# A 31-tap depthwise convolution: from shifted diagonals to four taps stacked on TensorE's rows, in four 32-column tiles

## The chip, the cores and the metric

One core of one Trainium2 chip runs the whole program. The time is the device time of one execution in microseconds, the median of three runs; the profile is one more execution, taken by the hardware profiler.

## The reference

Two transformer-like blocks run over 256 positions (rows) of 1024 channels, all in float32: first a convolution module and a mixture of 16 experts, then attention and a second mixture of experts, then a second block with its own branches. The change sits in the first module, near the start of the program:

```python
def conformer_conv(x, w_pw1, b_pw1, w_dw, b_dw, g, b, w_pw2, b_pw2):
    h = x @ w_pw1 + b_pw1                      # 256 x 1024 -> 256 x 2048
    a, gate = jnp.split(h, 2, axis=-1)
    h = a * jax.nn.sigmoid(gate)
    h = lax.conv_general_dilated(h, w_dw[:, None, :], window_strides=(1,),
        padding=[(CONV_WIDTH - 1, 0)], ..., feature_group_count=D_MODEL) + b_dw   # CONV_WIDTH = 31
    h = jax.nn.silu(layer_norm(h, g, b))
    return h @ w_pw2 + b_pw2                   # 1024 -> 1024
```

The convolution is depthwise: every channel is filtered over time with 31 taps of its own. Nothing behind it can start before it, since the layer norm needs the mean over all 1024 channels.

## The kernel before, in words

Channels lie on the 128 partitions in eight chunks (`c` = 0 to 7), time on the free axis: `hpad[:, c, :]` holds 30 zeros and the 256 gated values of chunk c, `conv[:, c, :]` the result.

Dense products (`split_product`) run in three terms of reduced-precision float32: ScalarE (ACT) copies half a weight block into `w_hi` (`high`), VectorE (DVE) or GpSimd (POOL) makes the remainder `w_lo` (`low`), and TensorE (PE) multiplies high by high, low by high, high by low. `("pw1", kind, half)` are the four blocks of the first matrix, a or g (gate) for channel chunks 0 to 3 (half 0) or 4 to 7 (half 1); PE takes them as a 0, g 0, a 1, g 1. Each block has two row halves `hb`; the third term of row half hb waits for `low(..., hb)`. `gate(half)` is ACT's sigmoid, `glu(half, n)` DVE's product that writes `hpad`; `("pw2", n)` are the blocks of the second matrix.

The 31 taps are shared. DVE does all 31 taps of chunks 0 to 3 and the first 21 of chunk 4 (`tap`: one `scalar_tensor_tensor` of 128 x 256, both tensors in SBUF), the first ten rounds while PE still multiplies block g 1, with the two `low` of that block between them at j = 4 and j = 6. PE does chunks 5, 6, 7 and the last ten taps of chunk 4: for each tap ACT builds a 128 x 128 diagonal matrix (`diagonal`, six buffers), and PE multiplies it with the shifted `hpad` and accumulates in PSUM, 103 matmuls in float32. Then PE averages over the channels (`conv_mean`, eight matmuls with a constant matrix), DVE centres, PE and ACT make the variance, DVE and ACT normalise and apply SiLU, and the product with pw2 follows.

Each engine runs its own instructions in the order written; waits are on semaphores. SP issues the weight loads in the order of the blocks (`stream`, `experts`), POOL loads parameters and the gain rows `rows` of the layer norms, and fetches `shifted` (the attention biases, made in this time too) out of DRAM. The expert stage behind loads 48 blocks of 2 MB, and its loads wait for buffers that the conv stage uses (`conv_over`).

## Time and profile before

| what | value |
|---|---|
| median of 3 runs | 1281.21 us (1279.31 to 1283.12) |
| span of the profiled execution, first to last instruction | 1275.6 us |
| time around the span, taken from the two rows above | 5.6 us |
| PE busy, share of the span | 1195.1 us, 94% |
| DVE, ACT, POOL busy | 50%, 37%, 16% |
| the convolution, from PE's first tap to the end of the channel mean | 63.6 to 112.05 us |

The profiler gives the span of its execution; the time around it is the difference to the median. Times in the views are counted from the start of the span. A float32 matmul leaves two records on PE and two weight loads (PEld), so 103 taps are x206. A row says when a group of instructions started and how long it took from its first start to its last end, how many they were, and in brackets how long the engine had been idle and who ended that.

### The profile page before, as it was taken

The numbers are of one execution on the slowest core, as the hardware profiler recorded it, in microseconds if no ns is written. First come the engines' busy times: TensorE is split into PE (matmuls) and PEld (weight loads), VectorE is DVE, ScalarE is ACT, GpSimd is POOL, SyncE is SP. The second block draws the span as 40 slices with busy tenths as digits, with TensorE's granted clock in tenths as the row PEclk, the third lists the DMA queues.
The fourth block names the chain that finished last, engine by engine and source line by source line (L and its number), as shares of the span: only waits on it lengthen the run. The fifth ranks groups of instructions, "written<-read, shape, count | busy, mean of one in ns | idle before, by whom it ended". The sixth has DMA issues, their size and how long they took to land.

```text
span 1275.6 us, 16095 instructions
## 1 busy us (share of the span) xinstructions
PE 1195.1 (94%) x6536; PEld 854.7 (67%) x6536; DVE 642.8 (50%) x949; ACT 478.1 (37%) x741; POOL 207.0 (16%) x190
## 2 busy tenths in 40 slices
PE   7998999999988998999999988999999889999998
PEld 7986754344435986654444435889887767988996
DVE  3897631212125678712222116596489885445544
ACT  3596421111103466311010113475566534444442
POOL 6000000000002000000000000087788550000000
PEclk9999989999999999789999998999999999999999
DMA  9900879999998531789999993533334342264450
GB/s 332 331 1 1 332 294 431 426 428 428 426 420 280 195 140 59 292 371 427 427 428 427 428 406 130 198 132 133 132 136 176 140 144 79 119 238 159 181 215 33
DMA packets 68162, 321.23 MB, mean 252 GB/s; under 512 B 4071, under 2 KB 12660, under 8 KB 55418
## 3 DMA queue, kind: packets, MB, share of 16 engines
q1 hardware_dynamic: 64944, 308.57, 61.1%
q0 software_dynamic: 2592, 11.42, 2.6%
q8 instruction: 52, 0.85, 0.3%
q10 hardware_dynamic: 554, 0.23, 0.1%
q14 instruction: 20, 0.16, 0.0%
HBM read 317.02 MB, written 3.18 MB: 251 GB/s over the span
## 4 chain that ended last, share of the span: by engine, by line
PE 70%; DVE 15%; DMA 5%; ACT 4%; issue 3%; POOL 2%; DVEq 0%; SPq 0%; ACTq 0%
PE bank L1529 32%; PE bank L1712 23%; PE bank L1594 4%; PE bank L1703 3%; DMA arena<-in_moe_w_up_dram 2%; POOL w_lo L666 2%; DMA ring<-in_w_kv_dram 2%; PE bank L1761 2%; DVE w_lo L666 2%; PE bank L1497 1%; ACT w_hi L953 1%; DVE arena L2298 1%; DVE rows L2852 1%; DVE arena L2871 1%; PE bank L1601 1%
## 5 line engine op out<-in xcount | busy, mean ns | idle before, releaser
L666 POOL TENSOR_TENSOR w_lo<-ring,w_hi 128x512 fp32r<-128x512 f32 (+1 forms) x124 | 178.1, 1469 | 659.3 <-ACT w_hi L953 659.3
L953 ACT ACTIVATE w_hi<-ring 128x2048 fp32r<-128x2048 f32 (+1 forms) x102 | 191.9, 1883 | 213.0 <-PE bank L1529 211.5
L666 DVE TENSOR_TENSOR w_lo<-ring,w_hi 128x2048 fp32r<-128x2048 f32 x71 | 160.8, 2266 | 150.4 <-ACT w_hi L953 149.9
L1529 PE MATMUL bank<-x_hi,w_hi 128*128 128x256 f32 x672 | 112.0, 289 | 3.9 <-DVE x_lo L2253 2.2
L1529 PE MATMUL bank<-x_hi,w_lo 128*128 128x256 f32 x672 | 108.9, 284 | 1.2 <-POOL w_lo L666 1.0
L1529 PE MATMUL bank<-x_lo,w_hi 128*128 128x256 f32 x672 | 108.3, 284 | 0.0
L1529 PE MATMUL bank<-w_hi,x_hi 128*128 128x512 f32 (+1 forms) x336 | 96.7, 403 | 10.8 <-DVE x_lo L2633 3.6
L1712 PE MATMUL bank<-arena 128*64 128x512 f32 x352 | 98.6, 594 | 1.9 <-ACT arena L953 1.8
L1529 PE MATMUL bank<-w_lo,x_hi 128*128 128x512 f32 (+1 forms) x336 | 94.4, 396 | 4.3 <-POOL w_lo L666 4.3
L1529 PEld LDWEIGHTS bank<-x_hi,w_hi 128*128 128x128 f32 x672 | 93.2, 193 | 6.5 <-issue 6.0
L953 ACT ACTIVATE arena<-bank 128x512 f32<-128x512 f32 (+3 forms) x85 | 40.0, 486 | 148.5 <-PE bank L1745 103.9
L2504 DVE TENSOR_TENSOR y_r<-bank,y_r 128x512 fp32r<-128x512 f32 x32 | 22.1, 691 | 143.6 <-ACT y_r L953 143.6
L1529 PEld LDWEIGHTS bank<-x_hi,w_lo 128*128 128x128 f32 x672 | 93.0, 193 | 1.8 <-POOL w_lo L666 1.8
L1529 PE MATMUL bank<-w_hi,x_lo 128*128 128x512 f32 (+1 forms) x336 | 93.6, 394 | 0.0
L1529 PEld LDWEIGHTS bank<-x_lo,w_hi 128*128 128x128 f32 x672 | 93.0, 192 | 0.0
L1712 PE MATMUL bank<-ring,arena 128*64 128x512 f32 x288 | 84.8, 594 | 7.1 <-ACT arena L953 7.1
L1712 PE MATMUL bank<-ring,moe_x 128*64 128x512 f32 x288 | 84.8, 594 | 1.3 <-DMA arena<-in_moe_w_up_dram 1.3
L1529 PEld LDWEIGHTS bank<-w_hi,x_hi 128*128 128x128 f32 x336 | 62.3, 196 | 24.3 <-issue 6.8
L1529 PEld LDWEIGHTS bank<-w_lo,x_hi 128*128 128x128 f32 x336 | 63.7, 195 | 20.3 <-POOL w_lo L666 7.7
L2530 DVE SCALAR_TENSOR_TENSOR arena<-arena,small,bank 128x512 f32<-128x512 f32 x16 | 17.7, 1105 | 116.9 <-PE bank L1712 116.9
L1529 PEld LDWEIGHTS bank<-w_hi,x_lo 128*128 128x128 f32 x336 | 64.5, 196 | 13.4
L2515 DVE TENSOR_TENSOR res<-res,bank 128x512 f32<-128x512 f32 x56 | 34.7, 682 | 74.5 <-PE bank L1761 74.5
(333 smaller groups left out, 1776.9 us busy)
## 6 DMA issues: line engine op xcount, KB each, us to landing
ring<-in_w_in_dram SPq DMA_DIRECT2D x15, 2048.0 KB, 7.8
ring<-in_moe_w_gate_dram SPq DMA_DIRECT2D x12, 2048.0 KB, 20.0
arena<-in_moe_w_down_dram SPq DMA_DIRECT2D x12, 2048.0 KB, 21.8
arena<-in_moe_w_gate_dram SPq DMA_DIRECT2D x12, 2048.0 KB, 17.1
ring<-in_moe_w_down_dram SPq DMA_DIRECT2D x12, 2048.0 KB, 18.4
ring<-in_moe_w_up_dram SPq DMA_DIRECT2D x12, 2048.0 KB, 17.6
arena<-in_moe_w_up_dram SPq DMA_DIRECT2D x12, 2048.0 KB, 21.4
wslots<-in_moe_w_up_dram SPq DMA_DIRECT2D x8, 2048.0 KB, 22.5
```

The source lines that it names most:

```text
L666: last = ops.tensor_tensor(part(w_lo, label, hb)[:, x].bitcast(F32R), ring_half(label, hb)[:, x], part(w_hi, label, hb)[:, x], ALU.subtract)
L953: return s.activation(dst, src, ACT.Copy)
L1497: mm(bank(label)[:, 0:cols], ident[:], moving[:, 0:cols], start=True, stop=True)
L1529: last = mm(bank(use_)[:, at:at + cols], still, moving, start=start and opens and (hb, n, k) == (0, 0, 0), stop=stop and closes and (hb, n ...
L1594: ins = mm(bank(("tap", c))[:, 0:T], diag[:, i % DIAGS, :], hpad[:, c, j:j + T], start=first, stop=last_)
L1601: ins = mm(bank(name)[:, 0:T], mean_w[:], src[:, k, :], start=first and k == channels[0], stop=last_ and k == channels[-1])
L1703: last = mm(b[:, i * width:(i + 1) * width], rows_[:, t, c * P:(c + 1) * P].bitcast(F32R), sel[:, t, :].bitcast(F32R), start=(n, t) == (0, ...
L1712: last = mm(b[half * CAP:(half + 1) * CAP, :], still(k)[:, half * CAP:(half + 1) * CAP], moving(half, k), start=k == 0, stop=k == k_range - 1)
L1761: last = mm(b, sel_T[:, buf, t * P:(t + 1) * P].bitcast(F32R), y[:, h * HALF:(h + 1) * HALF].bitcast(F32R), start=n == 0, stop=n == 1)
L2504: return v.tensor_tensor(y_lo[:, cols].bitcast(F32R), b, y_hi[:, cols], ALU.subtract)
L2515: ins = v.tensor_tensor(res[:, t, cols], res[:, t, cols], b, ALU.add)
L2530: free(v.scalar_tensor_tensor(hidden_rows(hx[:, 0, :]), by_hidden(sg[:, 0, :]), slot_gates[:, u % 2, :], by_hidden(bank(("up", l, u))[:]), ...
```

## The change

Chunks 2 to 7 go to PE, chunks 0 and 1 stay on DVE. PE no longer uses diagonals of 128 channels for one tap: the 128 rows of the array hold four taps (`STACK`) of 32 channels, and one group of 32 channels (g) is computed by one matmul with 32 output columns, written to PSUM partitions 32 g to 32 g + 31. Eight steps q of four taps make 32 taps (the last one zero), four groups g make 128 channels: 32 matmuls for a chunk, 192 in all. For this the moving data must hold the same 32 channels four times, shifted by 0, 1, 2 and 3 positions, on the four quarters of the partitions. SP writes `hpad[:, c, :]` to a DRAM buffer `gated` and reads it back with four DMAs for each chunk. The stationary matrices (128 x 1024 for a chunk, four diagonals of 32 under each other for each q and g) are made by POOL with one `tensor_tensor` each, from `strips` (0/1 pattern) and the tap column `wcol`. ACT's 103 diagonals are gone. The two `low` of the first pw2 block go from behind the channel mean to behind DVE's last tap, POOL's loads of `b2row` and `rows` to behind the last chunk's taps, and `wstack` (the taps in stacked layout) comes in with eight small DMAs and is transposed by PE in two more matmuls. Several semaphores are shared where there were two; nothing else is computed differently.

```diff
-PE_CHUNKS = (5, 6, 7)
-DIAGS = 6
-TAPS_AHEAD = 10
+DVE_CHUNKS = (0, 1)
+PE_CHUNKS = (2, 3, 4, 5, 6, 7)
+TAPS_AHEAD = 16
+STACK = 4
+STRIP = P // STACK
+STEPS = 8
+PADDED = CONV - 1 + T + 2
+REACH = T + STACK * (STEPS - 1)
...
@@ SP
+            stream(0, 3)
+            for q in range(STEPS):
+                n = min(STACK, CONV - STACK * q)
+                sp.dma_start(wstack[q % 4 * STRIP:q % 4 * STRIP + STRIP, q // 4, 0:n * STRIP]...)
+            stream(3, 5)
+            def shift_gated(c):
+                if c > 4:
+                    sp.wait_ge(sem(f"moved{c % 3}"), 16 * STACK)
+                for j in range(STACK):
+                    sp.dma_start(shifted_rows(c)[j * STRIP:(j + 1) * STRIP],
+                                 bass.AP(gated, c * PADDED + j, [[KD * PADDED, STRIP], [STRIP * KD * PADDED, STACK],
+                                                                 [1, REACH]])).then_inc(sem(f"moved{c % 3}"), 16)
+            sp.wait_ge(sem("glu"), 2)
+            keep_gated(2, 2, "gated_even")
+            sp.wait_ge(sem("gated_even"), 16)
+            for c in (2, 3):
+                shift_gated(c)
+            stream(5, moe_n[0])
+            for c, signal in ((4, "gated_even"), (5, "gated_odd")):
+                sp.wait_ge(sem("glu"), c + 1)
+                keep_gated(c, 1, signal)
+            ready(sp, ("pw1", "g", 1, 1))
+            for c in (4, 5, 6, 7):
+                signal = "gated_odd" if c % 2 else "gated_even"
+                sp.wait_ge(sem(signal), 16 * (c // 2 - c % 2))
+                shift_gated(c)
+                if c < 6:
+                    sp.wait_ge(sem("glu"), c + 3)
+                    keep_gated(c + 2, 1, signal)
@@ POOL
+            pool.wait_ge(sem("table_ahead"), 2)
+            freed(pool, "taps")
+            for c in PE_CHUNKS:
+                g.tensor_tensor(stacked(c), strips[:].unsqueeze(1).unsqueeze(1).broadcast_to([P, STEPS, STACK, STRIP]),
+                                wcol[:, :, c, :].unsqueeze(3).broadcast_to([P, STEPS, STACK, STRIP]), ALU.mult)\
+                    .then_inc(sem("stacked"), 1)
             pool.wait_ge(sem("lines"), 16)
...
+            ready(pool, ("tap", PE_CHUNKS[-1]))
+            par(b2row, a["a_b_pw2"].broadcast_to([P, D]), "par_b2")
+            load_rows(0)
+            load_rows(1)
@@ ACT
-            for i in range(DIAGS):
-                diagonal(i)
             highs(("pw1", "g", 1))
             high(("pw2", 0), 0)
             gate(1)
-            for i in range(DIAGS, len(PE_TAPS)):
-                diagonal(i)
...
+            high(("pw2", 0), 1)
+            for c in PE_CHUNKS:
+                tapped(c)
@@ PE
+            for n, c in enumerate(PE_CHUNKS):
+                claim(pe, ("tap", c))
+                pe.wait_ge(sem("stacked"), n + 1)
+                pe.wait_ge(sem(f"moved{c % 3}"), 16 * STACK * (2 if c > 4 else 1))
+                for q in range(STEPS):
+                    for g in range(STACK):
+                        last = mm(bank(("tap", c))[g * STRIP:(g + 1) * STRIP, 0:T], stacked(c)[:, q, g, :],
+                                  shifted_rows(c)[:, g, STACK * q:STACK * q + T], start=q == 0, stop=q == STEPS - 1)
+                full(last, ("tap", c))
+                if n:
+                    freed(pe, ("tap", PE_CHUNKS[n - 1]))
+                    over_channels("conv_mean", conv, (PE_CHUNKS[n - 1],), first=n == 1)
@@ DVE
-            for n in range(4):
+            for n in (2, 3, 0, 1):
                 glu(0, n)
...
             for j in range(TAPS_AHEAD):
                 if j == 4:
                     low(dve, v, ("pw1", "g", 1), 0)
-                if j == 6:
+                if j == 8:
                     low(dve, v, ("pw1", "g", 1), 1)
-                for c in range(4):
+                for c in DVE_CHUNKS:
                     tap(c, j)
```

PE's rows around the convolution, before (the taps are `bank<-arena 128x256`, the mean and variance the row with `mean_w`):

```order
L1529 MATMUL bank<-x_lo,w_hi 128x256 x4
L1529 MATMUL bank<-x_hi,w_lo 128x256 x4
L1594 MATMUL bank<-arena 128x256 x103
L1601 MATMUL bank<-arena,mean_w 128x256 x16
L1610 MATMUL bank<-arena 128x512 x4
L1497 MATMUL bank<-blockmask,ident 128x512 x4
L1529 MATMUL bank<-w_hi,x_hi 128x512 x4
```

and in the changed kernel, where the stationary matrices lie in `rows` and `res` and the shifted data in `arena` and `x_rep`:

```order
L1584 MATMUL bank<-x_hi,w_lo 128x256 x4
L1666 MATMUL bank<-arena,rows 32x256 x64
L1648 MATMUL bank<-arena,mean_w 128x256
L1666 MATMUL bank<-x_rep,rows 32x256 x32
L1648 MATMUL bank<-arena,mean_w 128x256
L1666 MATMUL bank<-x_rep,rows 32x256 x32
L1648 MATMUL bank<-arena,mean_w 128x256
L1666 MATMUL bank<-x_rep,res 32x256 x32
L1648 MATMUL bank<-arena,mean_w 128x256
L1666 MATMUL bank<-arena,res 32x256 x32
L1648 MATMUL bank<-arena,mean_w 128x256 x4
L1648 MATMUL bank<-res,mean_w 128x256 x8
```

103 matmuls of 128 columns have become 192 of 32 columns, and the mean's matmul for a chunk now stands behind the next chunk's taps.

DVE's rows from the first gated product on, before (`L2298` are taps, `L666` the `low` of a block half):

```order
L2280 SCALAR_TENSOR_TENSOR arena<-bank,pcol,arena 128x256 x4
L2287 COPY small<-eps_ln 128x1 x2
L2294 TENSOR_SCALAR arena<-arena,pcol 128x256 x4
L2298 SCALAR_TENSOR_TENSOR arena<-arena 128x256 x12
L666 TENSOR_TENSOR w_lo<-ring,w_hi 128x2048
L2298 SCALAR_TENSOR_TENSOR arena<-arena 128x256 x8
L666 TENSOR_TENSOR w_lo<-ring,w_hi 128x2048
L2298 SCALAR_TENSOR_TENSOR arena<-arena 128x256 x16
L2280 SCALAR_TENSOR_TENSOR arena<-bank,pcol,arena 128x256 x4
L2287 COPY small<-eps_ln 128x1 x2
L2298 SCALAR_TENSOR_TENSOR arena<-arena 128x256 x4
L2294 TENSOR_SCALAR arena<-arena,pcol 128x256
L2298 SCALAR_TENSOR_TENSOR arena<-arena 128x256 x100
```

and in the changed kernel (`L2354` taps, `L689` `low`):

```order
L2336 SCALAR_TENSOR_TENSOR arena<-bank,pcol,arena 128x256 x4
L2343 COPY small<-eps_ln 128x1 x2
L2350 TENSOR_SCALAR arena<-arena,pcol 128x256 x2
L2354 SCALAR_TENSOR_TENSOR arena<-arena 128x256 x6
L689 TENSOR_TENSOR w_lo<-ring,w_hi 128x2048
L2354 SCALAR_TENSOR_TENSOR arena<-arena 128x256 x8
L689 TENSOR_TENSOR w_lo<-ring,w_hi 128x2048
L2354 SCALAR_TENSOR_TENSOR arena<-arena 128x256 x16
L2336 SCALAR_TENSOR_TENSOR arena<-bank,pcol,arena 128x256 x4
L2343 COPY small<-eps_ln 128x1 x2
L2354 SCALAR_TENSOR_TENSOR arena<-arena 128x256 x30
L689 TENSOR_TENSOR w_lo<-ring,w_hi 128x2048 x2
```

Eight taps stand ahead of the first `low` where there were sixteen (the first taps of a chunk are the `TENSOR_SCALAR` rows), 62 taps in all for 145; the last two `low` are those of pw2.

POOL's rows behind its small parameter loads, before:

```order
L877 DMA kg<-in_k_norm_g_dram 128x64
L877 DMA hng<-in_hgrn_norm_g_dram 128x128
L894 DMA rows<-in_ln_mix_g_dram 128x1024
L894 DMA rows<-in_ln_mix_b_dram 128x1024
L894 DMA rows<-in_ln_ffn_g_dram 128x1024
L894 DMA rows<-in_ln_ffn_b_dram 128x1024
L902 DMA arena<-bias_lines 128x8x256 x2
L908 DMA biases<-arena 128x4096
```

and in the changed kernel (the first two rows are the stationary matrices of six chunks):

```order
L941 DMA hng<-in_hgrn_norm_g_dram 128x128
L963 TENSOR_TENSOR rows<-strips,arena 128x1024 x4
L963 TENSOR_TENSOR res<-strips,arena 128x1024 x2
L969 DMA arena<-bias_lines 128x8x256 x2
L941 DMA arena<-in_a_b_pw_dram 128x1024
L957 DMA rows<-in_ln_mix_g_dram 128x1024
L957 DMA rows<-in_ln_mix_b_dram 128x1024
L957 DMA rows<-in_ln_ffn_g_dram 128x1024
L957 DMA rows<-in_ln_ffn_b_dram 128x1024
L980 DMA biases<-arena 128x4096
```

The six products stand ahead of the two reads of `bias_lines`, and the loads of `rows` behind them.

## Rows read from the trace of the kernel before

**Rows 1.** The page: span, and TensorE's busy time.
```profile
span 1275.6 us, 16095 instructions
PE 1195.1 (94%) x6536; PEld 854.7 (67%) x6536; DVE 642.8 (50%) x949; ACT 478.1 (37%) x741; POOL 207.0 (16%) x190
```

**Rows 2.** Chain that ended last, in order: start us, us, what.
```profile
63.56 45.01 PE bank L1594 x206
108.58 3.47 PE bank L1601 x16
...
114.01 5.39 PE bank L1601 x16
...
124.22 2.20 DVE w_lo L666
126.42 1.22 DVE x_lo L2346 x2
...
127.68 11.22 PE bank L1529 x48
```

**Rows 3.** Timeline of DVE, 37 to 63 us: start, us.
```profile
41.24 1.66 DVE L2280 SCALAR_TENSOR_TENSOR arena<-bank,pcol,arena 128x256 f32<-128x256 f32 x4
...
44.36 4.83 DVE L2298 SCALAR_TENSOR_TENSOR arena<-arena 128x256 f32<-128x256 f32 x12
49.11 2.29 DVE L666 TENSOR_TENSOR w_lo<-ring,w_hi 128x2048 fp32r<-128x2048 f32 x1
...
54.49 2.28 DVE L666 TENSOR_TENSOR w_lo<-ring,w_hi 128x2048 fp32r<-128x2048 f32 x1
```

**Rows 4.** Timeline of PE's weight loads and matmuls in block g 1.
```profile
51.45 0.53 PEld L1529 LDWEIGHTS bank<-x_hi,w_lo 128*128 128x128 f32 x4
...
61.62 0.64 PE L1529 MATMUL bank<-x_hi,w_lo 128*128 128x256 f32 x4
```

**Rows 5.** Timeline of ACT: copies of the taps and of the bias line.
```profile
41.71 0.83 ACT L953 ACTIVATE arena<-bank 128x248 f32<-128x248 f32 x2
```

**Rows 6.** Timeline, POOL alone, then POOL and DVE together near 960 us.
```profile
390.73 1.27 POOL L666 TENSOR_TENSOR w_lo<-ring,w_hi 128x512 fp32r<-128x512 f32 x1 [246.60 <-ACT w_hi L953]
...
959.56 5.89 POOL L666 TENSOR_TENSOR w_lo<-ring,w_hi 128x512 fp32r<-128x512 f32 x4
...
961.49 2.82 DVE L2852 SCALAR_TENSOR_TENSOR rows<-rows,pcol 128x255 f32<-128x255 f32 x2
```

**Rows 7.** Groups of POOL by form, and its timeline: the shortest and the most broken patterns.
```profile
L666 POOL TENSOR_TENSOR w_lo<-ring,w_hi 128x68 fp32r<-128x68 f32 x4 | 1.2, 320 | 355.9 <-ACT w_hi L953 355.9
...
3.16 0.71 POOL L864 TENSOR_SCALAR_AFFINE_SELECT blockmask<-ones 128x128 f32<-128x128 f32 x1
...
11.46 0.29 POOL L864 TENSOR_SCALAR_AFFINE_SELECT blockmask<-ones 128x128 f32<-128x128 f32 x1
```

**Rows 8.** Windows: us, busy of PE, PEld, DVE, ACT, POOL, then the granted clock.
```profile
115.10:118.60 3.50, 3.50 (x11) 2.76 (x10) 2.16 (x2) 0.56 (x1) 0.00 (x0) 0.51 0.00 0
```

**Rows 9.** Timeline and chain: matmuls with 64 columns, and with 128 columns.
```profile
192.45 0.61 PE L1712 MATMUL bank<-ring,arena 128*64 128x512 f32 x1 [0.89 <-ACT arena L953]
...
192.45 0.64 PE L1712 MATMUL bank<-arena 128*64 128x512 f32 x1
...
175.25 13.91 PE bank L1712 x64
...
119.23 3.60 PE L1610 MATMUL bank<-arena 128*128 128x512 f32 x8
```

**Rows 10.** DMA issues: KB each, us from issue to landing.
```profile
out_dram<-res SPq DMA_DIRECT2D x2, 512.0 KB, 2.7
...
arena<-bias_lines POOLq DMA_DIRECT2D x2, 1024.0 KB, 8.0
```

**Rows 11.** Timeline of ACT in the normalisation: the second of four roundings.
```profile
125.22 0.63 ACT L953 ACTIVATE x_hi<-arena 128x512 fp32r<-128x512 f32 x1
```

**Rows 12.** The chain at the end of the first expert stage.
```profile
363.30 25.01 DMA ring<-in_w_kv_dram
```

More of the change, by code:

```diff
@@ L151, in program @@
         w_lo = [sb(f"w_lo{i}", [P, BLK // 2]) for i in range(2)]
+        with nc.sbuf_tensor("x_rep", [P, 3, STACK, REACH], F32) as x_rep:
+            pass
         x_hi = sb("x_hi", [P, KD, T])
@@ L186, in program, with shifted_rows, stacked @@
         wdw = take(CONV * KD)
+        wcol = take(STEPS, KD, STACK)
+        rep_first = take(2, STACK, REACH)
+        assert take.at[0] <= 3 * BLK
+        def shifted_rows(c):
+            return rep_first[:, c - 2] if c < 4 else x_rep[:, c - 4] if c < 7 else rep_last[:, 0]
+        def stacked(c):
+            where = (rows[0][:, 0, :], rows[0][:, 1, :], rows[1][:, 0, :], rows[1][:, 1, :], res[:, 0, :], res[:, 1, :])
+            return where[c - 2].rearrange("p (q g m) -> p q g m", q=STEPS, g=STACK)
         take = carve(3 * BLK)
@@ L325, in program @@
         over_any = [sb(f"over_any{l}", [1, 1], I32) for l in range(LAYERS)]
+        gated = nc.dram_tensor("gated", (P, KD, PADDED), F32, kind="Internal")
         lines = nc.dram_tensor("bias_lines", (2 * HEADS, BIAS_LINE), F32, kind="Internal")
@@ L1576, in _ @@
             for n in range(2):
-                last = tr(bank("taps")[:, n * 124:(n + 1) * 124], wst[0:124, n, :], ident[0:124, 0:124])
+                tr(bank("taps")[:, n * 124:(n + 1) * 124], wst[0:124, n, :], ident[0:124, 0:124])
+            pe.wait_ge(sem("par_stack"), 16 * STEPS)
+            pe.wait_ge(sem("hpad0"), 3)
+            for n in range(2):
+                last = tr(bank("taps")[:, (2 + n) * P:(3 + n) * P], wstack[:, n, :], ident[:])
             full(last, "taps")
@@ L2320, in _ @@
             for j in range(TAPS_AHEAD, CONV):
-                for c in range(4):
+                for c in DVE_CHUNKS:
                     tap(c, j)
-                tap(4, j - TAPS_AHEAD)
-            dve.wait_ge(sem("conv_tap"), DVE_TAPS)
-            ready(dve, ("tap", 4))
-            free(v.tensor_tensor(conv[:, 4, :], conv[:, 4, :], bank(("tap", 4))[:, 0:T], ALU.add), ("tap", 4))
-            freed(dve, ("tap", 4))
+            low(dve, v, ("pw2", 0), 0)
+            low(dve, v, ("pw2", 0), 1)
             ready(dve, "conv_mean")
@@ L2333, in _ @@
                 ins.then_inc(sem("conv_centred"), 1)
-            low(dve, v, ("pw2", 0), 0)
             dve.wait_ge(sem("conv_centred"), 4)
```

117 lines of the change are left out of this document (48 added, 69 removed).

## The prediction

> **What bounds the kernel now.** I read the page first: PE is busy for 1195.1 of 1275.6 us [rows 1]. So a change pays where it takes time out of PE's own queue, or out of a wait there. Then the chain that ended last, for the place of the change: it lies on PE. From 63.56 us PE works 45.01 us on the taps, 206 records for 103 matmuls, 0.437 us each, then 3.47 us on the channel mean [rows 2]. The end of the mean at 108.58 + 3.47 = 112.05 us is what I compare below; everything behind it hangs on it. Third, the timelines of DVE and PE ahead of the taps. PE's product g 1 stands between two suppliers: its third term begins at 51.45 us, right when DVE's `low`, begun at 49.11 us for 2.29 us, is ready, and its last matmuls end at 61.62 + 0.64 = 62.26 us [rows 3, 4]. So that `low` has no slack before the change either. That is the place to watch.
>
> **The taps on PE.** The change removes 49.8 us (62.26 to 112.05) of waiting, taps and mean. It puts in 192 matmuls of 32 columns on four column tiles. The trace has none of these; it has matmuls of 64 columns on two tiles. There the first matmuls of the two tiles start at the same 192.45 us, and a pair of products, 64 records, takes 13.91 us: 32 matmuls of 512 columns, 0.435 us each. With the full width the same form takes 3.60 us for 8 records, 0.90 us each [rows 9]. So two column tiles truly run side by side. If four do too, a step q costs the 0.43 us of one matmul: 48 x 0.43 = 20.6 us. If only two did, it would be 192 x 0.43 / 2 = 41.3 us. I take 20.6, since the only tiled row scales fully, and keep 41.3 as the far end. With the eight matmuls of the mean (3.5 us) the stretch is 24.1 us, so 25.7 us less than 49.8.
>
> A rule speaks for a dearer value: the Trainium skill (TensorE: Matmul & The Clock Gate, Part 3 on packing small matmuls) gives 2.38 times for three column tiles, 79% of full scaling; by it, as an estimate, the taps would cost 20.6 / 0.79 = 26 us and the sum would be 5.5 us higher. No row here shows three or four tiles; the two-tile rows show no such loss.
>
> **The stationary matrices on POOL.** Six `tensor_tensor` of 1024 columns. POOL alone takes 1.27 us for 512 columns [rows 6] and 0.32 us for 68 [rows 7], so 2.14 ns a column, and 2.37 us for 1024. The pattern is broken into 32 runs of 32; the first mask (64 runs) takes 0.71 us where the last (one run) takes 0.29 [rows 7], 7 ns a run, so 0.2 us more: 2.6 us. The far end is that mask's 5.5 ns a column, 5.7 us. I take 2.6, the same operation. They start when ACT has copied the taps, 41.71 + 0.83 = 42.54 us [rows 5].
>
> By themselves they are hidden: 6 x 2.6 us end at 58, and PE wants the first at 62. But DVE works beside them on operations with two SBUF tensors. Near 960 us the same two engines meet: four POOL operations take 5.89 us, 1.47 each instead of 1.27, and two DVE `scalar_tensor_tensor` of 255 columns take 2.82 us, 1.41 each [rows 6], where a tap of this form takes 4.83 / 12 = 0.40 [rows 3]. I read that as turns: one DVE operation gets in between two POOL operations, and each waits for the other. With POOL operations twice as long, DVE then does one tap per 2.6 + 0.2 = 2.8 us, not seven. Operations that read PSUM are not of this kind, so the gated products (from 41.24 us, 1.66 us for four [rows 3]) pass.
>
> The sum on DVE: POOL is done at 42.54 + 2.6 + 5 x 2.8 = 59.1 us. By then DVE has five taps. Taps 6, 7, 8 need 1.2 us, and `low` for g 1 another 2.3 us: ready at 62.6 us. PE stands in its third term from 51.45 us until then: **+11.1 us**. In the queue behind it are all of g 1, the taps and the mean. DVE's second `low` comes 3.2 + 2.3 us later, at 68.1, when PE is 4.8 + 1.0 us into the rest: just in time. The two added transposes of the taps on PE (under 0.5 us) vanish in this wait.
>
> After a wait PE's clock falls: behind the gap at 112 us the granted clock is 0.51 for 3.5 us [rows 8], the lower level of 1.2 GHz, and sixteen records take 5.39 us where sixteen of the same form took 3.47 [rows 2]. The longer wait here will do the same once: **+1.9 us**. Block g 1 ends at 62.26 + 11.1 + 1.9 = 75.3 us, then **-25.7 us** for the stretch: the mean ends at 99.4 us, not 112.05.
>
> **Input through DRAM.** For each chunk SP issues one write and four reads of 147 KB. 512 KB take 2.7 us to land in a quiet stretch [rows 10]. Chunks 2 and 3 go out at about 42.5 us, early. Chunk 4 waits for the first gated product of half 1, behind DVE's 32 taps: 62.6 + 3.2 + 2.3 + 16 x 0.40 = 74.5 us; write 2.7, reads issued 1.6 and landed 2.7 later: 81.5 us. PE has chunks 2 and 3 until 75.3 + 6.9 = 82.2 us. Cost nothing, with under 1 us to spare. Chunks 5 to 7 follow about every 2 us and PE takes 3.9 us for each. If that cover went, a landing of 8.0 us as `bias_lines` had under load [rows 10] in both directions would cost 10 us. DVE's last 30 taps (12.1 us from 77) and the two `low` (4.6 us) end near 94, ahead of the mean's last part.
>
> **ACT, and behind the mean.** ACT's 103 diagonals fed PE's taps and delayed nothing else; taking them out is worth nothing of its own. Behind the mean one `low` of 2.20 us stands on the chain at 124.22, and PE starts 1.22 us after it at 127.68 [rows 2]; with it gone, DVE's second remainder follows ACT's rounding at 125.22 + 0.63 us [rows 11] and is done near 126.5: **-1.1 us**. The loads for the expert stage start with the layer norm's end and PE's progress and move along; where that stage ends on its queue (25.01 us of DMA on the chain [rows 12]) the queue has moved as well, so the gain is kept.
>
> **Sum.** 11.1 + 1.9 - 25.7 - 1.1 = -13.8 us. The profiled span of 1275.6 us becomes 1261.8; with the 5.6 us between span and median, 1281.2 - 13.8 = **1267.4 us**.
>
> **The rivals.**
> - *DVE is not held by POOL*, or gets more than one turn: then `low` is ready before 50 us, g 1 ends at 62.7 with the two transposes, and chunk 4's data land at 61.7 + 2.7 + 1.6 + 2.7 = 68.7, ahead of PE's 69.6. The mean ends at 86.8: -25.2 - 1.1, **1254.9 us**. For it: the row near 960 us is another stage. Against it: its two engines run the same kinds of operation.
> - *Column tiles run two at a time*: +20.7 us, **1288.1 us**, slower than before. It decides from 0.72 us for a step of four on, where 0.43 is full scaling. For it: more than two are not shown. Against it: both start within one record, with nothing lost.
> - *POOL's broken pattern is dear*: each 1 us of its price costs 6 us; from 4.9 us on the gain is gone, and at 5.7 us the time is **1286 us**.
> - *The way through DRAM is late*, or the tiles scale by three quarters: 5 to 10 us more, **1272 to 1278 us**.
>
> **How the numbers follow.** Forecast 0.57 (its own range 1262 to 1272), no hold 0.16, late data or partly scaled tiles 0.14, two tiles at a time 0.08, dear POOL 0.05. Leaving out the last two, the range is 1254 to 1279 us. The measurement tells about 0.3%, 4 us, from no change. Faster by more: 0.57 + 0.16 + nearly all of 0.14 and little else, 0.86; within it 0.03; slower 0.11.
>
> **What would show it.** The third term of g 1 starts near 62.6 us, its PE wait named by DVE's `w_lo`; DVE's taps last 2.5 us and more while POOL makes the matrices, 0.48 us after; POOL's six take 2.6 to 2.8 us each; a chunk's 64 records on PE take 3.4 us; a granted clock of 0.5 for some 3.5 us once g 1 goes on; no wait on `x_rep` from DMA beyond 1 us. Taps at 0.48 us throughout would break the largest term; 7 us for a chunk would break the gain; a wait of PE for DMA at chunk 4 would move the loss to the DRAM route.

## The result, and the profile after

The changed kernel takes 1264.47 us in the median of four runs (1263.55 to 1264.67); the kernel before, run on the same chip beside it, takes 1280.26 us (1279.02 to 1283.12). The ratio is 0.987, with a 95% interval of 0.986 to 0.989: 15.8 us less. The forecast was 1267.4 us, 13.8 us less.

The page after, to be set against [rows 1]:

```profile
span 1262.9 us, 16324 instructions
...
PE 1178.5 (93%) x6716; PEld 829.4 (66%) x6716; DVE 619.0 (49%) x866; ACT 441.4 (35%) x642; POOL 218.9 (17%) x198
```

The span falls from 1275.6 to 1262.9 us, 12.7 us, and PE's busy time by 16.6. The profiled execution after has a device time of 1264.65 us, 1.75 us around its span. In the executions of the kernel before that were timed beside the experiments, 1.7 to 2.7 us lie around the span. So the 5.6 us "around the span" in the table before were in good part scatter: the profiled execution before was a quick one, some 2 to 3 us below the median. That is also most of the step from 12.7 us between the traces to 15.8 us between the medians. The sums below are made from span to span, as the prediction's was.

The timelines of DVE and POOL while the stacked matrices are made (start us, us, engine, line, operation, how many), against [rows 3]:

```profile
42.63 7.81 POOL L963 TENSOR_TENSOR rows<-strips,arena 128x1024 f32<-128x1024 f32 x4 [22.59 <-ACT arena L1025]
50.41 4.14 POOL L963 TENSOR_TENSOR res<-strips,arena 128x1024 f32<-128x1024 f32 x2
...
43.90 2.72 DVE L2350 TENSOR_SCALAR arena<-arena,pcol 128x256 f32<-128x256 f32 x2
46.54 9.08 DVE L2354 SCALAR_TENSOR_TENSOR arena<-arena 128x256 f32<-128x256 f32 x6
55.54 2.28 DVE L689 TENSOR_TENSOR w_lo<-ring,w_hi 128x2048 fp32r<-128x2048 f32 x1
...
60.91 2.28 DVE L689 TENSOR_TENSOR w_lo<-ring,w_hi 128x2048 fp32r<-128x2048 f32 x1
63.12 6.42 DVE L2354 SCALAR_TENSOR_TENSOR arena<-arena 128x256 f32<-128x256 f32 x16
```

Two windows of about 4 us show the exchange (busy time and number of PE, PEld, DVE, ACT, POOL, those at the edges counted in, then the granted clock): three operations of DVE for three of POOL, then eleven where POOL is silent.

```profile
50.55:54.50 3.95, 1.10 (x10) 0.90 (x8) 3.95 (x3) 1.62 (x1) 3.95 (x3) 1.00 1.03 284
63.20:67.20 4.00, 4.00 (x36) 4.00 (x35) 4.00 (x11) 1.92 (x1) 0.00 (x0) 1.00 0.17 60
```

POOL's six products take 11.9 us, about 2.0 each, and DVE's taps keep step with them, where from 63.12 us on a tap takes 0.40 us. POOL's operations are shorter than forecast (2.0 us instead of 2.6), so `low` is ready at 57.8 us and not at 62.6.

The timeline of PE, against [rows 2] and [rows 4]; the bracket is the idle time before the group and who ended it:

```profile
57.88 1.23 PE L1584 MATMUL bank<-x_hi,w_lo 128*128 128x256 f32 x4 [6.23 <-DVE w_lo L689]
...
70.23 7.11 PE L1666 MATMUL bank<-arena,rows 128*32 128x256 f32 x128
...
77.90 3.66 PE L1666 MATMUL bank<-x_rep,rows 128*32 128x256 f32 x64
...
97.68 3.69 PE L1648 MATMUL bank<-res,mean_w 128*128 128x256 f32 x16 [1.53 <-ACT res L1150]
...
108.61 1.21 PE L1584 MATMUL bank<-w_hi,x_hi 128*128 128x512 f32 x4 [0.37 <-DVE x_lo L2397]
```

The wait for `w_lo` is there, 6.2 us long. Between the taps there is no wait for the transfers. The chain gives the parts of the stretch without overlap:

```profile
70.30 7.04 PE bank L1666 x128
77.34 0.63 PE bank L1648 x2
77.97 3.59 PE bank L1666 x64
...
94.22 1.94 PE bank L1648 x8
```

The mean is done at 94.22 + 1.94 = 96.16 us, 15.9 us earlier than the 112.05 of before (forecast 99.4). A window over the wait and what follows (busy time of PE, PEld, DVE, ACT, POOL, then the granted clock, the DMA share and GB/s) shows the price of the pause:

```profile
51.00:65.00 14.00, 7.77 (x52) 7.57 (x51) 14.00 (x19) 2.01 (x2) 5.32 (x4) 0.76 0.94 314
```

The last place to read is late. The two programs are the same from the layer norm on, yet the lead is not kept:

| place, on PE | before | after | lead |
|---|---|---|---|
| end of the mean | 112.05 | 96.16 | 15.9 |
| first product of pw2 | 127.68 | 108.61 | 19.1 |
| first expert product | 175.25 | 156.11 | 19.1 |
| third pair of expert products | 220.52 | 203.14 | 17.4 |
| last mixing of the first expert stage | 391.70 | 375.90 | 15.8 |
| next dense product | 406.29 | 393.63 | 12.7 |

Two pairs of expert products ran in part at the lower clock (15.65 and 15.38 us instead of 13.95), which is nearly all of the first 3.3 us. The other 3.1 us are lost in one place. Here are the same instructions of the kernel before and then of the one after, the 16 warming matmuls in front of the next layer norm's transposes:

```profile
391.70 2.11 PE L1761 MATMUL bank<-y_r,selT_r 128*128 128x512 f32 x8 [1.99 <-DVE y_r L2504]
394.38 7.13 PE L1497 MATMUL bank<-blockmask,ident 128*128 128x512 f32 x16 [0.57 <-DVE res L2515]
402.19 1.07 PE L1645 MATMUL bank<-ident,xtok 128*128 128x128 f32 x8 [0.67 <-DVE xtok L2405]
```

```profile
375.90 2.10 PE L1815 MATMUL bank<-y_r,selT_r 128*128 128x512 f32 x8 [1.61 <-DVE y_r L2555]
381.38 8.80 PE L1552 MATMUL bank<-blockmask,ident 128*128 128x512 f32 x16 [3.38 <-issue]
390.01 1.91 PE L1699 MATMUL bank<-ident,xtok 128*128 128x128 f32 x16
```

Before, the warming matmuls follow 0.57 us behind the mixing and are over when the transposes' data arrive at 402.19. After, PE stands still for 3.38 us with no releaser ("issue"). The matmuls then take 8.80 us instead of 7.13: the granted clock reads 1.00 when they start and 0.53 from 382.4 to 386.0 us. The transposes wait behind them: the data of the first ones had been there since 386.6 us, of the others since 388.0.

### The profile page after: what moved, and what is told of

Read it like the earlier page. It is cut to its first block, busy times and chain, and to the rows that moved or that the text cites. A ratio compares the mean times of both kernels' runs of the same rounds, so it can differ in the third digit from the quotient of the medians.

```text
span 1262.9 us, 16324 instructions
## 1 busy us (share of the span) xinstructions
PE 1178.5 (93%) x6716; PEld 829.4 (66%) x6716; DVE 619.0 (49%) x866; ACT 441.4 (35%) x642; POOL 218.9 (17%) x198
## 4 chain that ended last, share of the span: by engine, by line
PE 72%; DVE 15%; ACT 5%; issue 3%; DMA 3%; POOL 2%; DVEq 0%; SPq 0%; ACTq 0%
PE bank L1584 34%; PE bank L1766 25%; PE bank L1757 3%; DMA arena<-in_moe_w_up_dram 2%; PE bank L1815 2%; POOL w_lo L689 2%; PE bank L1666 2%; DVE w_lo L689 1%; PE bank L1552 1%; ACT w_hi L1025 1%; DVE rows L2903 1%; DVE arena L2581 1%; DVE arena L2922 1%; DVE arena L2354 1%; PE bank L1799 1%
## 5 line engine op out<-in xcount | busy, mean ns | idle before, releaser
L689 POOL TENSOR_TENSOR w_lo<-ring,w_hi 128x512 fp32r<-128x512 f32 (+1 forms) x124 | 178.1, 1469 | 663.9 <-ACT w_hi L1025 663.9
L689 DVE TENSOR_TENSOR w_lo<-ring,w_hi 128x2048 fp32r<-128x2048 f32 x71 | 160.8, 2267 | 149.2 <-ACT w_hi L1025 148.7
L1766 PE MATMUL bank<-arena 128*64 128x512 f32 x352 | 103.3, 613 | 1.9 <-ACT arena L1025 1.8
L1766 PE MATMUL bank<-ring,arena 128*64 128x512 f32 x288 | 87.9, 606 | 7.1 <-ACT arena L1025 7.1
L1025 ACT ACTIVATE arena<-bank 128x512 f32<-128x512 f32 (+4 forms) x86 | 40.3, 486 | 148.5 <-PE bank L1799 103.5
```

Source lines behind the costliest of these rows:

```text
L689: last = ops.tensor_tensor(part(w_lo, label, hb)[:, x].bitcast(F32R), ring_half(label, hb)[:, x], part(w_hi, label, hb)[:, x], ALU.subtract)
L1025: return s.activation(dst, src, ACT.Copy)
L1766: last = mm(b[half * CAP:(half + 1) * CAP, :], still(k)[:, half * CAP:(half + 1) * CAP], moving(half, k), start=k == 0, stop=k == k_range - 1)
```

## The experiments

Each is an edit of the changed kernel. A shift of 1.5 to 2.7 us can lie over all times of one execution, because the six records of PE's first three warming matmuls (at 11.3 us, 17.3 us in experiment 8) took 2.81 us in some executions and 4.3 to 5.5 us in others; where it matters I say so. Where it comes from stands in the last section.

**1. The low parts first.**

```diff
-                if j == 4:
+                if j == 0:
                     low(dve, v, ("pw1", "g", 1), 0)
-                if j == 8:
+                if j == 1:
                     low(dve, v, ("pw1", "g", 1), 1)
```

> Edit: both low(pw1,g,1) stand ahead of nearly all of VectorE's taps (the first at tap 0, the second after two taps) instead of after 8 and 16. Theory A (GpSimd's six products hold VectorE's taps, and what TensorE waits for is only the low part queued behind eight held taps): TensorE's idle 6.2 us before the first x_hi,w_lo matmuls of pw1 g1 is under 1 us, half 1 of pw1 g ends near 62.5 instead of 70.3, and the clock stays at 1.00 through it. But VectorE still has its 32 taps ahead of the gates of half 1, so these come near 68.3 (69.5 now); with 0.5 us to the write, 2.5 us for it, and 4 us for issue and read, chunk 4's rows land near 74 to 75 while TensorE is done with chunks 2 and 3 at 69.6. So TensorE waits some 4 to 5 us there, and the mean comes only about 3 us earlier: near 1261.5 us. Theory B (the DRAM route has slack to spare, or the wait is given back nowhere): the whole 7.8 us, near 1256.7. Theory C (POOL holds VectorE whatever the order is, the low part itself comes late): no gain, 1264.5.

1266.89 us (1264.14 to 1272.69), ratio to the kernel before 0.989 (0.986 to 0.992). The timeline of DVE, then of PE:

```profile
46.61 3.88 DVE L689 TENSOR_TENSOR w_lo<-ring,w_hi 128x2048 fp32r<-128x2048 f32 x1 [2.57 <-ACT w_hi L1025]
50.42 3.92 DVE L2350 TENSOR_SCALAR arena<-arena,pcol 128x256 f32<-128x256 f32 x2
54.26 4.00 DVE L689 TENSOR_TENSOR w_lo<-ring,w_hi 128x2048 fp32r<-128x2048 f32 x1
58.18 11.96 DVE L2354 SCALAR_TENSOR_TENSOR arena<-arena 128x256 f32<-128x256 f32 x30
70.06 1.65 DVE L2336 SCALAR_TENSOR_TENSOR arena<-bank,pcol,arena 128x256 f32<-128x256 f32 x4
```

```profile
63.30 7.11 PE L1666 MATMUL bank<-arena,rows 128*32 128x256 f32 x128
77.26 5.81 PE L1666 MATMUL bank<-x_rep,rows 128*32 128x256 f32 x64 [6.21 <-DMA x_rep<-gated]
```

The taps start at 63.30 instead of 70.23 us: what PE had waited for was only the low part's place behind held taps, as theory A says. And the wait comes back at chunk 4, 6.2 us for the rows out of DRAM. That was to be 4 to 5 us; the gates come at 70.06 and not at 68.3 because the low parts are held too, 3.9 us each instead of 2.28. Behind the wait the chunk takes 5.81 instead of 3.66 us, so the mean ends at 95.66 + 1.99 = 97.7 us, 1.5 later than in the changed kernel. Theories B and C fall. The gain of about 3 us that I expected is not there: in the trace it is a loss of 1.5 us, in the times no difference (the intervals overlap).

**2. The low parts first, and fewer taps ahead of the gates.**

```diff
-TAPS_AHEAD = 16
+TAPS_AHEAD = 8
```
(and the edit of experiment 1)

> Edit: as the run before, and TAPS_AHEAD is 8 instead of 16, so that VectorE does 16 taps and not 32 before the gates of half 1. Theory A: the gates come near 62 to 63, chunk 4's rows land near 68.5, before TensorE asks for them at 69.6; VectorE's remaining 46 taps of 0.40 us end near 83 to 84, before the mean asks at 88. The mean ends near 88.3 instead of 96.15, all of 7.8 us is kept: near 1256.7 us. Rival: if it is the writes and reads through DRAM, not VectorE's queue, that makes TensorE wait in the run before, the wait at chunk 4 stays over 3 us and the time stays near 1261.

1260.61 us (1257.40 to 1263.86), ratio 0.984 (0.981 to 0.987). PE's timeline:

```profile
11.22 4.73 PE L1552 MATMUL bank<-xtok,ident 128*128 128x512 f32 x6 [1.57 <-DVE x_lo L2301]
...
65.08 7.11 PE L1666 MATMUL bank<-arena,rows 128*32 128x256 f32 x128
...
72.92 3.66 PE L1666 MATMUL bank<-x_rep,rows 128*32 128x256 f32 x64
...
89.17 1.99 PE L1648 MATMUL bank<-arena,mean_w 128*128 128x256 f32 x8
```

No wait over 0.2 us is left between the taps, so it was DVE's queue ahead of the gates that made the rows late. The mean ends at 91.2 us, 5.0 earlier than in the changed kernel although this execution lost 4.73 - 2.81 = 1.9 us at its start: 6.9 of the 7.8 us expected. The times show less than the trace: the median lies 3.9 us above the 1256.7 us expected, and its interval still touches that of the changed kernel (0.986 to 0.989).

**3. POOL's products in halves.**

```diff
-                g.tensor_tensor(stacked(c), ...)
+                for h in range(2):
+                    steps = slice(h * STEPS // 2, (h + 1) * STEPS // 2)
+                    ins = g.tensor_tensor(stacked(c)[:, steps], ...)
```

> Edit: GpSimd builds each stacked matrix in two products of 512 columns instead of one of 1024 (12 in all); nothing else. Theory A (VectorE passes by turns, one of its instructions for each of GpSimd's): GpSimd's total stays near 11.8 us (12 of 0.98), VectorE's taps in that stretch take about 1.1 us each instead of 2.1, the eight ahead of the low part are done near 52 to 52.5 instead of 55.5, the low part near 54.8, TensorE's wait is 3.2 instead of 6.2 us and the time about 3 us less: near 1261.5. Rival (VectorE is held in proportion to GpSimd's busy time, whatever the size of its instructions): the taps stay at 2.1 us, the low part at 57.8, no change within 0.5 us of 1264.5. Third: a fixed cost of an instruction of GpSimd of 0.5 us or more would lengthen its total to 17 us, and the stacked matrices would still be early enough (needed from 70.3 on).

1262.91 us (1260.46 to 1270.04), ratio 0.988 (0.984 to 0.992): the time alone tells nothing. The timelines do:

```profile
42.47 8.94 POOL L966 TENSOR_TENSOR rows<-strips,arena 128x512 f32<-128x512 f32 x8 [20.35 <-ACT arena L1028]
...
45.65 7.22 DVE L2357 SCALAR_TENSOR_TENSOR arena<-arena 128x256 f32<-128x256 f32 x6
52.79 3.13 DVE L689 TENSOR_TENSOR w_lo<-ring,w_hi 128x2048 fp32r<-128x2048 f32 x1
```

```profile
55.97 1.22 PE L1587 MATMUL bank<-x_hi,w_lo 128*128 128x256 f32 x4 [4.49 <-DVE w_lo L689]
```

Six taps take 7.22 us, 1.2 each, where a held tap took 2.0, and the first eight of POOL's halves 1.12 us each. The taps follow the length of POOL's instruction, as turns do, so the rival falls. The low part begins 2.75 us earlier, but it is now itself among POOL's work (3.13 us instead of 2.28): PE's wait is 4.49 us, between the two expected values.

**4. The order of the tiles.**

```diff
-                for q in range(STEPS):
-                    for g in range(STACK):
+                for g in range(STACK):
+                    for q in range(STEPS):
```

> Edit: in each chunk the loops over the column tiles and the steps are swapped: eight matmuls in a row on one 32-column tile, then the next, instead of the four tiles in turn. The matmuls are the same. Theory T (the 0.11 us a matmul of the 4-tile taps comes from four neighbouring matmuls running at once on different tiles): in a row on one tile each takes the 0.43 us that a full-width matmul of 256 columns takes; a chunk goes from 3.5 to 13 to 14 us, six chunks from 21 to some 80, and the time rises by about 58 to 62 us, to near 1325. Rival (a matmul of 32 columns is just cheaper by itself, its price goes with the stored columns): no change, 1264.5. Between: overlap only at the changes of tile, 3 of 31, near 1320.

1311.22 us (1309.24 to 1313.19), ratio 1.024 (1.020 to 1.028). PE's timeline:

```profile
70.05 21.98 PE L1666 MATMUL bank<-arena,rows 128*32 128x256 f32 x128
...
92.59 11.50 PE L1666 MATMUL bank<-x_rep,rows 128*32 128x256 f32 x64
```

The same 32 matmuls take 11.50 instead of 3.66 us when neighbours share a tile. That is the overlap of the four tiles, a factor of 3.1 (3.5 if the three changes of tile in this order overlap fully), and the rival falls. Over six chunks 68.0 us instead of 21.4 are 46.6 more, and the time rose by 46.8. My 58 to 62 us were too much: in a row on one tile a 32-column matmul takes 0.36 us (0.40 if the three changes of tile overlap fully), not the 0.437 of a full-width tap [rows 2].

**5. The mean behind all taps.**

```diff
             for n, c in enumerate(PE_CHUNKS):
                 ...
-                if n:
-                    freed(pe, ("tap", PE_CHUNKS[n - 1]))
-                    over_channels("conv_mean", conv, (PE_CHUNKS[n - 1],), first=n == 1)
             pe.wait_ge(sem("conv_tap"), DVE_TAPS)
-            over_channels("conv_mean", conv, DVE_CHUNKS)
+            over_channels("conv_mean", conv, DVE_CHUNKS, first=True)
+            for c in PE_CHUNKS[:-1]:
+                freed(pe, ("tap", c))
+                over_channels("conv_mean", conv, (c,))
```

> Edit: the mean's matmuls of chunks 2 to 6 stand behind all the taps instead of between them. Theory S (each change between 32-column tiles and full-width matmuls costs time: two matmuls of the mean took 0.63 us between chunks and eight in a row 1.94, which is 0.49 for two, and a chunk of taps behind a mean 3.59 instead of 3.52): the stretch from the first tap to the mean's end, 25.9 us now, is 21.1 of taps and 3.9 of 16 mean matmuls, 25.0: 0.9 us less. Rival (the 0.63 is only where the modelled ends fall, nothing is lost at a change): 25.9 as before, within 0.1. Either way the time of the whole, 1264.5, moves by less than its noise of some 2 us; the stretch in the trace decides.

1264.95 us (1263.46 to 1266.53), ratio 0.988 (0.986 to 0.991). PE's timeline:

```profile
73.44 7.11 PE L1666 MATMUL bank<-arena,rows 128*32 128x256 f32 x128
...
94.30 3.72 PE L1648 MATMUL bank<-arena,mean_w 128*128 128x256 f32 x16
```

From the first tap to the mean's end are 98.02 - 73.44 = 24.6 us instead of 25.9: 1.3 us less, where 0.9 was expected. The taps take 20.9 instead of 21.4 us and the mean 3.7 instead of 4.5. A change between 32-column tiles and full width costs time on both sides. (This execution lost 2.7 us at its start.)

**6. The low parts of pw2 back behind the mean.** The edit puts `low(("pw2", 0), 0)` behind the centring and `low(("pw2", 0), 1)` behind the normalising, where the kernel before has them:

```diff
-            low(dve, v, ("pw2", 0), 0)
-            low(dve, v, ("pw2", 0), 1)
             ready(dve, "conv_mean")
             ...
+            low(dve, v, ("pw2", 0), 0)
             dve.wait_ge(sem("conv_centred"), 4)
             ...
+            low(dve, v, ("pw2", 0), 1)
```

> Edit: the two low parts of pw2's first block go back to where the kernel before had them, one behind the centring, one behind the normalising. Theory 1 (the prediction's term): the first one lies in VectorE's 3.1 us of waiting for the deviation and costs nothing, the second stands ahead of the first x_lo and delays pw2's first split matmul (108.6 now) by 1.1 to 1.4 us; the variance matmuls stay at 3.7 us for 16 at a clock of 1.00, because the gap ahead of them is 1.5 us in both. Theory 2 (the move is also what kept the clock up at the variance): the 16 variance matmuls go back to 5.4 us and pw2 starts 3 us later. The time: 1265.7 by the one, 1267.5 by the other.

1266.58 us (1264.20 to 1270.38), ratio 0.990 (0.987 to 0.992). PE's timeline:

```profile
98.91 3.69 PE L1648 MATMUL bank<-res,mean_w 128*128 128x256 f32 x16 [1.53 <-ACT res L1150]
...
110.89 1.21 PE L1584 MATMUL bank<-w_hi,x_hi 128*128 128x512 f32 x4 [1.42 <-DVE x_lo L2397]
```

pw2's first product waits 1.42 instead of 0.37 us: 1.05 us is what the move is worth, close to the 1.1 of the prediction. The variance still takes 3.69 us, so theory 2 falls.

**7. All three edits** (experiments 2 and 5 together).

> Edit: the low parts first, 16 VectorE taps ahead of the gates instead of 32, and the mean behind the taps, together: the candidate for a version better than both. From the second run's profile, whose mean ended at 91.16 in an execution that began 1.8 us late on TensorE, minus 0.9 if the changes of tile cost what theory S says: the mean ends at 90.3 with that late start and at 88.5 without. Against 96.15 that is 5.9 to 7.7 us less, and the time, 1260.6 in the second run, would be 1257 to 1260.

1260.94 us (1257.11 to 1267.57), ratio 0.988 (0.984 to 0.991), the profiled execution with a span of 1255.4 us. PE's timeline:

```profile
73.50 7.15 PE L1666 MATMUL bank<-x_rep,rows 128*32 128x256 f32 x128 [1.43 <-DMA x_rep<-gated]
...
87.67 3.72 PE L1648 MATMUL bank<-arena,mean_w 128*128 128x256 f32 x16
```

The mean ends at 91.4 us with a late start of 1.9, against 90.3 expected, and the median lies just above the 1257 to 1260 us expected. The gain of experiment 5 is gone into a new wait: without the mean's matmuls between chunks PE asks for chunk 4's rows sooner, and waits 1.43 us for them.

**8. More instructions ahead on PE.** 24 matmuls of 16 columns on the identity, results unused, before the input has landed:

```diff
+            claim(pe, ("x", 0))
+            for _ in range(24):
+                mm(bank(("x", 0))[:, 0:16], ident[:], ident[:, 0:16], start=True, stop=True)
             pe.wait_ge(sem("x_in"), 16)
```

> Edit: 24 matmuls of 16 columns on the identity before the input has landed, in TensorE's first 6 us of idle time, so that all of its later instructions lie further on in its program; nothing else. The question is the 2.9 us for which no releaser shows in the first layer, behind the last expert and the branch over the spill (ahead of the 16 warming matmuls at 381.4), which all five profiles of the changed program have (2.8 to 3.8 us) and the one of before has not. Theory F (it hangs on where the code behind the branch lies): the idle time changes clearly, to under 1 us or to more than 4, and the warming matmuls run at full clock, 7.1 instead of 8.8 us, if it goes. Theory G (it hangs on what the DMA queues or the other engines do at that time): it stays at 2.8 to 3.8 us. The time: 1264.5 if it stays, some 1261 if it goes. The added matmuls hide behind the 6 us wait for the input and cost nothing; if the first transposes run at a higher clock for them, a further 1 us goes.

1269.22 us (1267.64 to 1272.27), ratio 0.992 (0.990 to 0.995). PE's timeline:

```profile
1.78 10.42 PE L1612 MATMUL bank<-ident 128*128 128x16 f32 x48 [1.78 <-POOL ident L901]
...
383.55 7.13 PE L1552 MATMUL bank<-blockmask,ident 128*128 128x512 f32 x16 [0.57 <-DVE res L2569]
```

The matmuls do not hide: 48 records at 0.217 us are 10.4 us, and pw2 starts 5.9 us later than in the changed kernel. But the stall is gone: 0.57 us and 7.13 us, to the hundredth as before the change, and of the 5.9 us only 2.1 are left at the next dense product (395.74 against 393.63).

**9. The same with 9 matmuls.**

> Edit: as the run before with added matmuls, but 9 of them instead of 24. In that run the 24 matmuls came to 48 instructions of 0.217 us, 10.4 us and not under 6, which pushed everything up to pw2 back by 5.9 us; of the 5.9 only 2.1 were left at 395 us, because the 2.9 us of idle time ahead of the warming matmuls was gone (0.57 us, as before the change) and these ran in 7.1 instead of 8.8 us. With 9, 18 instructions of 0.217 us end at 5.7 us, before the input at 6.1: no delay. Theory F1 (any sufficient shift of the code behind the branch removes the stall, 36 instructions of weights and matmuls with it): idle 0.57 us, all behind it 3.6 us earlier, near 1261. Theory F2 (the shift is too short, or the 96 instructions of the other run were needed to cross a boundary): the stall stays at 2.8 us and the time at 1264.5. Theory G (the stall went in that run because of the 4 to 6 us shift in time against the transfers, and not in code): it stays too, so only its going tells F1 from both others.

1265.54 us (1264.20 to 1266.62), ratio 0.987 (0.986 to 0.989). PE's timeline:

```profile
382.41 8.80 PE L1552 MATMUL bank<-blockmask,ident 128*128 128x512 f32 x16 [4.30 <-issue]
```

The stall stays, and with it the time of the changed kernel. So not every shift of the code removes it, or it was the shift in time that did it in experiment 8.

**10. The best version that the runs suggested:** the low parts first, `TAPS_AHEAD = 6`, the mean behind the taps, and the 9 matmuls of experiment 9.

> Edit: the low parts first, 12 VectorE taps ahead of the gates (TAPS_AHEAD 6; with 16 ahead TensorE waited 1.4 us for chunk 4's rows once the mean stood behind the taps), the mean behind the taps, and the 9 added matmuls of the run beside this one. Expected: gates 1.6 us earlier than with 8 ahead, no wait at chunk 4, the mean's end at 88.5 (full clock from the start) to 90.5; and, if the stall ahead of the warming matmuls goes, 3.6 us more behind it. The time: 1257 to 1259 without the last, 1253 to 1256 with it; before was 1279 to 1281 and the changed kernel 1264.5.

1258.59 us (1257.55 to 1263.22), ratio 0.982 (0.981 to 0.984), an interval that lies below that of the changed kernel. The time is in the 1257 to 1259 us expected for a stall that stays. PE's timeline:

```profile
74.04 7.11 PE L1669 MATMUL bank<-x_rep,rows 128*32 128x256 f32 x128 [1.90 <-DMA x_rep<-gated]
...
376.26 8.80 PE L1552 MATMUL bank<-blockmask,ident 128*128 128x512 f32 x16 [2.87 <-issue]
```

Both hopes behind this version failed: the stall stays, and PE still waits 1.90 us at chunk 4, though the first gates come 1.5 us earlier (63.86 instead of 65.38 in experiment 7). In the groups of DMA issues the writes `gated<-arena` of this stretch now take 4.2 us to land (median of four), 3.3 in experiment 7, and SP issues chunk 4's reads at 69.28 instead of 68.85 us: what DVE gains, the writes lose.

**11. The 24 matmuls inside PE's own wait.** They stand in the changed kernel's 6.2 us of idle time, in front of the third term of g 1:

```diff
+                        if n == 2 and (label, hb, opening) == (("pw1", "g", 1), 0, True):
+                            freed(pe, ("pw1", "a", 0, 0))
+                            for _ in range(24):
+                                mm(bank(("pw1", "a", 0, 0))[:, 0:16], ident[:], ident[:, 0:16], start=True, stop=True)
                         if n == 2 and opening:
                             pe.wait_ge(lo_made[hb], ...)
```

> Edit: the 24 added matmuls of 16 columns (48 instructions on TensorE) stand in the changed kernel's 6.2 us of idle time ahead of the first x_hi,w_lo of pw1's g1, instead of ahead of the input. They take 0.1 us each there at full clock, 5 us, so nothing is put back, but all code behind them lies exactly as far on as in the run with 24 that lost the 2.9 us stall, and the times of the transfers are those of the changed kernel. Theory F2 (where the code lies decides, and 9 more matmuls were too few): idle ahead of the 16 warming matmuls 0.57 us instead of 3.4, these at 7.1 instead of 8.8 us, pw2's products of the next stage from 390.0 instead of 393.6. Theory G (it was the 6 us shift in time against the transfers): the stall stays at 2.8 us or more. Beside it: if TensorE is kept busy through the wait, the clock stays at 1.00 and the half of pw1's g1 behind the wait takes 10.8 instead of 12.4 us; taps begin at 68.7 instead of 70.3. The time: 1264.5 minus 1.6 for the clock, minus 3.6 more by F2: near 1259.5, or near 1263 by G.

1265.17 us (1259.72 to 1267.64), ratio 0.987 (0.984 to 0.990). PE's timeline:

```profile
53.46 7.78 PE L1581 MATMUL bank<-ident 128*128 128x16 f32 x48
...
376.63 3.43 PE L1819 MATMUL bank<-y_r,selT_r 128*128 128x512 f32 x8 [1.99 <-DVE y_r L2559]
379.98 7.34 PE L1552 MATMUL bank<-blockmask,ident 128*128 128x512 f32 x16
```

The stall is gone again, with the last mixing at 376.63 us where the changed kernel has 375.90. A shift in time against the transfers, 0.7 us here, does not explain it, for the last mixing starts at 376.12 us in experiment 6, where the stall stays. The code's place is left, theory F2. The gain by it does not show in the time: the matmuls took 7.78 us instead of 5 and delayed the taps (74.13 us, with a late start of 1.9).

The second expectation of this run failed, and says more than the first. PE was busy through the whole former wait, and its granted clock fell all the same: it reads 1.00 until 56.2 us and 0.50 from there to 66.4. The added records follow each other every 0.112 us before that and every 0.214 us after it. The part of g 1 behind them takes 13.1 us (61.07 to 74.13), where 10.8 was expected and 12.4 is the changed kernel's after its 6.2 us of idle time. Matmuls of 16 columns back to back did not keep the clock up here.

**What PE waits for at the stall.** One part of the profile bears on it, the DMA queues. This is a line of the page of the changed kernel:

```profile
q8 instruction: 54, 0.88, 0.3%
```

This queue moves packets of 16 KB, one for about every 250 records of PE. Around the stall the trace has them at these times (us):

| version | mixing ends | 16 KB packet on q8 | warming matmuls start |
|---|---|---|---|
| changed kernel | 378.00 | 378.62 to 379.81 | 381.38 |
| experiment 1 | 378.73 | 378.81 to 379.91 | 381.50 |
| experiment 9 | 378.11 | 379.74 to 380.84 | 382.41 |
| kernel before | 393.81 | 395.68 to 396.79 | 394.38 |
| experiment 8 | 382.97 | 384.77 to 385.85 | 383.55 |
| experiment 11 | 380.06 | 380.71 to 381.81 | 379.98 |

In all ten versions with the stall PE goes on 1.57 to 1.60 us behind the end of such a packet. In the three without it PE goes on before the packet has started. So PE stands still until its next instructions are there. That the queue is PE's own is read from these distances and from the count of its packets; the view names no engine for it.

## Why the prediction was right, step by step

The direction, the mechanism and the size of the sum held. That the sum came so near is in part luck: several terms were off and cancelled.

- **DVE is held by POOL, one operation for one of POOL's.** Right. Six products, and DVE's taps stretched while they last, free afterwards; experiment 3 shows that the taps' price follows the length of POOL's instruction. The gated products, which read PSUM, passed as forecast: four in 1.66 us from 42.07 us on, the last two thirds of it beside POOL's first product, as without it [rows 3]. The rival without a hold (1254.9 us) is out. The rule did not say that a long DVE operation is held as well: `low` took 3.9 instead of 2.28 us in experiment 1.
- **POOL's price, 2.6 us a product, 2.8 a turn.** Mis-sized: 11.9 us for six, 2.0 a turn. The 0.2 us that I added for the broken pattern is not there, and the price from 512 columns was not to be scaled as I did. It made `low` late at 57.8 instead of 62.6 us, a delay of 6.4 us and not 11.1.
- **The clock's loss behind the wait, 1.9 us.** Measured 1.6: g 1 from 57.88 to 70.30 us is 12.4 us where it took 10.8 [rows 4].
- **The stretch of taps and mean, 24.1 us.** Measured 25.9. The taps' term (20.6) was nearly right, 21.4; experiment 4 shows that this is the overlap of four tiles. The missing part is the mean: 4.5 instead of 3.5 us, since each piece stands between 32-column work (experiment 5). The rival with two tiles at a time is out: in this form the four tiles lose 4% against the forecast. The Trainium skill (TensorE: Matmul & The Clock Gate, Part 3 on packing small matmuls) gives 2.38 times for three tiles, which is 79% of full scaling. As a ratio to the same matmuls in a row on one tile, this case's trace does not contradict it: 3.1 to 3.5 of 4, 79 to 87% (experiment 4). What failed is the 26 us that I worked out from it, since I set the 79% against the 0.43 us of a full-width matmul. A 32-column matmul in a row takes only 0.36 to 0.40 us, and so a step of four takes 0.45 us.
- **The way through DRAM is hidden.** Right, and the slack was about as thin as the sum said: when PE comes 7 us earlier (experiment 1, with the gates 0.6 us later) it waits 6.2 us there.
- **Behind the mean, -1.1 us.** The move of `low` is worth 1.05 us (experiment 6). But the lead grew by 3.2 us there, since the variance's 16 records took 3.7 instead of 5.39 us [rows 2]: the gap ahead of them was 1.53 us, where it had been 1.96, and the clock did not fall. Experiment 6 shows that the moved `low` is not why. All twelve versions of the changed kernel have the 1.53 us and the 3.7. The gap is shorter because DVE's centring starts 0.04 us behind the mean's end, where before it started 0.49 us behind it. Why it does, and whether the gap is what keeps the clock, stays open.
- **"The gain is kept" behind the expert stage.** This step failed. 6.4 of 19.1 us of lead are lost by 393 us: 3.3 mostly to two stretches at the lower clock, which not every profile has (in experiments 2 and 7 the same two pairs take 13.95 us), and 3.1 to the stall, in which PE waits for its instructions. The stall is in the changed kernel and in experiments 1 to 7, 9 and 10, and not in the two with 24 more matmuls. The prediction had no term for either.

From span to span the measured terms are 6.4 + 1.6 - 23.9 - 3.2 + 6.4 = -12.7 us; the forecast was 11.1 + 1.9 - 25.7 - 1.1 = -13.8. POOL's price (4.7 us too dear) and the variance (2.1) nearly made up for the stretch (1.8) and for what was lost late (6.4). From median to median the forecast of 1267.4 us is 2.9 us too high, since it carried the 5.6 us around the span, where 1.75 were measured.

## What to carry to other kernels

When GpSimd is given work beside VectorE, count its instructions, and look at what stands in VectorE's queue behind that many operations: the low part that TensorE wants belongs ahead of them. Then follow the queue one step further, since the next user (here the gates that feed a way through DRAM) inherits the delay; in the traces only moving both gave the gain. Small matmuls on separate column tiles pay nearly in full if neighbours in the queue are on different tiles, and a lead won early in a long program should be followed through to the end of the trace before it is counted.

## What the runs showed of the hardware

- Four 32-column tiles in turn: 3.66 us for 32 float32 matmuls of 256 columns; the same on one tile after the other 11.50 us.
- POOL and DVE beside each other, both with two SBUF tensors: taps of 0.40 us took 2.0 us beside products of 1024 columns and 1.2 beside 512; a `low` of 2.28 us took 3.9 to 4.0 us beside 1024 and 3.13 beside 512.
- Where code lies can cost 3 us: behind a branch, PE idled 2.8 to 4.3 us with no releaser in ten versions and 0.6 us or nothing in the kernel before and in two others, which differ from the changed one by 48 matmul records further up. In the ten it went on 1.57 to 1.60 us behind the end of a 16 KB packet on the queue that the profile calls q8 instruction.
- The first three warming matmuls took 2.81 us in six profiles and 4.3 to 5.5 in seven others. The views show a granted clock of 1.00 there in all of them, but that is no reading: the trace's first clock record begins only at 9.4 to 17.3 us, and the views print 1.00 where there is none. In the six it begins ahead of these matmuls, in the seven behind their start (14.2 to 17.3 us). The difference spreads over the whole execution and is as large as several of the terms studied here.
- Matmuls of 16 columns back to back: a record every 0.112 us at a granted clock of 1.00, every 0.214 us at 0.50 (experiment 11), and every 0.213 us in the first 12 us of experiment 8, ahead of the first clock record. Filling a wait with them did not keep the clock up.
